# Two attention stages of a hybrid decoder layer written as one stage

## The reference, cut to what matters

```python
def mla_attend(q_lat, q_pe, segments):
    scores = []
    for c_kv, k_pe, mask in segments:
        s = (einsum('bqhc,bkc->bhqk', q_lat, c_kv)
             + einsum('bqhr,bkr->bhqk', q_pe, k_pe)) * SOFTMAX_SCALE
        scores.append(where(mask, s, -inf))
    p = softmax(concatenate(scores, axis=-1), axis=-1)
    # out: the sum over the segments of p times c_kv
```

## Time and profile before

| | us |
|---|---|
| median of 3 runs | 1552.9 (1550.19 to 1553.53) |
| the profiled execution's own time | 1556.86 |
| its span in the trace | 1555.2 |
| PE busy | 1470.7 (95%) |
| DVE busy | 810.7 (52%) |
| ACT busy | 582.2 (37%) |
| POOL busy | 389.4 (25%) |

### The profile page before, as it was taken

One profiled execution on the slowest core, in us unless ns is written; L12 is line 12 of the kernel. 1 busy time (PEld: TensorE's weight loads), 2 busy tenths in 40 slices (PEclk: granted clock), 3 DMA queues, 4 the chain that ended last, 5 costly groups with the idle time before them and its releaser, 6 DMA issues. The chain is left out here.

```text
span 1555.2 us, 26517 instructions
## 1 busy us (share of the span) xinstructions
PE 1470.7 (95%) x9613; PEld 1253.4 (81%) x9613; DVE 810.7 (52%) x1466; ACT 582.2 (37%) x1264; POOL 389.4 (25%) x520
## 2 busy tenths in 40 slices
PE   5999999999989988888999999999999998999997
PEld 4997777676767866555888999999999998787786
DVE  4512200054456654333148665666656665698877
ACT  4521112122333433222044544455444444443454
POOL 1136631040033002433000543433444342000000
PEclk9999999998989998997999999999999999999999
DMA  6431223343335001563232323332233335754764
GB/s 228 148 106 49 98 104 129 104 142 97 121 93 137 1 1 54 145 184 96 84 114 68 95 85 107 108 107 79 79 99 108 108 108 181 250 189 160 256 222 162
DMA packets 143279, 186.79 MB, mean 120 GB/s; under 512 B 22931, under 2 KB 89732, under 8 KB 142998
## 3 DMA queue, kind: packets, MB, share of 16 engines
q1 hardware_dynamic: 138382, 175.68, 35.2%
q0 software_dynamic: 4800, 9.84, 2.3%
HBM read 149.25 MB, written 36.19 MB: 119 GB/s over the span
## 5 line engine op out<-in xcount | busy, mean ns | idle before, releaser
L2939 PE MATMUL p_ff<-s_ff_th,s_ff_rhi 128*128 128x266 f32 x640 | 182.9, 286 | 0.4 <-ACT s_ff_u L2523 0.4
L2941 PE MATMUL p_ff<-s_ff_tl,s_ff_rhi 128*128 128x266 f32 x640 | 183.0, 286 | 0.0
L2942 PE MATMUL p_ff<-s_ff_th,s_ff_rlo 128*128 128x266 f32 x640 | 183.0, 286 | 0.0
L2939 PE MATMUL p_ff<-s_xh,s_ff_rhi 128*128 128x266 f32 x608 | 175.6, 289 | 5.4 <-DVE s_ff_rlo L2710 2.7
L2941 PE MATMUL p_ff<-s_xl,s_ff_rhi 128*128 128x266 f32 x608 | 174.2, 286 | 0.0
L2942 PE MATMUL p_ff<-s_xh,s_ff_rlo 128*128 128x266 f32 x608 | 173.9, 286 | 0.0
L118 PE MATMUL p_ip<-s_ip_hi,s_xh 128*128 128x512 f32 (+2 forms) x400 | 149.8, 375 | 3.6 <-DVE s_xl L216 3.6
L120 PE MATMUL p_ip<-s_ip_hi,s_xl 128*128 128x512 f32 (+2 forms) x400 | 148.8, 372 | 0.0
L119 PE MATMUL p_ip<-s_ip_lo,s_xh 128*128 128x512 f32 (+2 forms) x400 | 148.7, 372 | 0.0
L3044 PE MATMUL p_ff<-s_fd_wh,s_fd_ah 128*128 128x512 f32 x308 | 123.3, 400 | 8.2 <-DVE s_fd_wl L2818 4.3
L2939 PEld LDWEIGHTS p_ff<-s_xh,s_ff_rhi 128*128 128x128 f32 x608 | 114.9, 189 | 15.5 <-DVE s_ff_rlo L2710 8.5
(11 more groups left out here) (316 smaller groups left out, 3126.4 us busy)
## 6 DMA issues: line engine op xcount, KB each, us to landing
s_ff_raw<-in_w_up SPq DMA_DIRECT2D x44, 512.0 KB, 4.7
s_fd_lanes<-in_w_down SPq DMA_DIRECT2D x77, 256.0 KB, 3.4
s_fd_lanes<-a_rows SPq DMA_DIRECT2D x66, 256.0 KB, 3.3
a_rows<-s_ff_cv SPq DMA_DIRECT2D x22, 512.0 KB, 3.0
s_ff_scr<-in_w_down SPq DMA_DIRECT2D x11, 1024.0 KB, 6.1
s_ip_raw<-in_w_in SPq DMA_DIRECT2D x4, 2048.0 KB, 8.8
s_pages<-in_cache_kv_latent SPq DMA_DIRECT2D x56, 128.0 KB, 2.3
s_pages<-in_cache_kv_latent POOLq DMA_DIRECT2D x48, 128.0 KB, 2.5
```

The costliest lines, as they stand in the source:

```text
L2939: pe.matmul(out, rhi[:, s, ks_], hi_cols(k), start=first and k == 0, stop=False, skip_group_check=True)
L2941: pe.matmul(out, rhi[:, s, ks_], lo_cols(k), start=False, stop=False, skip_group_check=True)
L2942: mm = pe.matmul(out, rlo[:, s, ks_], hi_cols(k), start=False, stop=last and k == 3, skip_group_check=True)
```

## The change: what it does, and the diff

The two functions become one, `attention`, with one loop over k = 0..35. In step k it handles prompt item k and, for k < 32, cache page k (of four sequences). The other parts:

- The softmax of decode runs over blocks of 4 pages (8 blocks, 4 for each group) where it ran over segments of 8. Each block has its own maximum, exponential and rescaling of `total`. In step 4(B+1) block B gets maximum and exponential, one step later its transposes and `weigh`, and one step after that `take_part`.
- The pages lie in one ring of 8. Page n is loaded once `out_done` is n - 7, that is when `weigh` has passed page n - 8.
- The rotary keys of two sequences are transposed together, 128 columns wide, and multiplied from rows 0 to 63 and 64 to 127 of the matrix engine: 10 transposes for a page where there were 12.
- PSUM: 4 score banks as before, a ring of two banks for all transposes of both kinds (before: two in one stage, three in the other), one bank for the block's scores, and one bank that holds the two outputs of the prompt items and the output of the decode block (`misc`).
- Scores of decode are computed for 128 columns at a time, before for 256.
- SP issues its small transfers, two of them for the rotary queries, ahead of the first page. The first half of w_out is loaded once `weigh` has passed page 31, in step 33.

```diff
+NPG = 8
+BP = 4
+NBLOCK = DEC_B * NPAGE // (GB * BP)
+PAGES = NBLOCK * BP
 ...
+def attention(kit, t, x, spill, ident, w_uk, w_uv, qn_s, qp_s, kn, vt, qn, qp, kp, mh, ml, room, pages):
 ...
+        ring_b = kit.ps(c, "at_turn", 2)
+        mix_b = kit.ps(c, "at_mix", 1)
+        block_b = kit.ps(c, "at_block", 1)
 ...
+                sp.wait_ge(R["kept"], 2)
+                sp.dma_start(qpe_other[0:RO], qp_s[RO:P]).then_inc(R["q_low"], 16)
+                sp.dma_start(qpe_other[RO:P], qp_s[0:RO]).then_inc(R["q_low"], 16)
+                sp.wait_ge(pages.table, 16)
+                for n in range(NPG):
+                    pages.load_sync(sp, n)
 ...
+                for n in range(NPG, PAGES):
+                    sp.wait_ge(R["out_done"], n - NPG + 1)
 ...
+                    pages.load_sync(sp, n)
 ...
+                for k in range(NI):                      # ScalarE
+                    if k < PAGES:
+                        empty(act, place["keys", k, 0], copy)
+                    if k + 1 < NI:
+                        exp_part(k + 1)
+                    if block_at(k, 0) is not None:
+                        block_exp(block_at(k, 0))
+                    if k < PAGES:
+                        empty(act, place["keys", k, 2], copy)
 ...
+                def page_scores(n):                      # TensorE
+                    B, p = divmod(n, BP)
 ...
+                    wait_left(pe, place["keys", n, 1])
+                    wait_left(pe, place["keys", n, 2])
 ...
+                    if p == 0 and B:
+                        pe.wait_ge(R["exped"], B)
 ...
+                def weigh(B):
 ...
+                    wait_left(pe, place["probs", B])
+                    pe.wait_ge(S["lo_out"], BP * (B + 1) + 1)
 ...
-                for i in range(len(items)):
-                    if i + 1 < len(items):
-                        score_part(i + 1)
-                    if i:
-                        value_part(i - 1)
-                    turn_part(i)
+                for k in range(NI):
+                    if k + 1 < NI:
+                        score_part(k + 1)
+                    if k < PAGES:
+                        fill(place["keys", k, 0])
+                        fill(place["keys", k, 1])
+                    if k:
+                        value_part(k - 1)
+                    if k < PAGES:
+                        fill(place["keys", k, 2])
+                    B = block_at(k, 1)
+                    if B is not None:
+                        fill(place["probs", B])
+                        if last_of_group(B):
+                            fill(place["own", B])
+                    for n in turns(k):
+                        fill(n)
+                    if k < PAGES:
+                        page_scores(k)
+                        if (k + 1) % (GBLOCKS * BP) == 0:
+                            fill(place["self", k // (GBLOCKS * BP)])
+                    if B is not None:
+                        weigh(B)
+                    if closed(k) is not None:
+                        fill(place["close", closed(k)])
+                    if k and closed(k - 1) is not None:
+                        head_values(closed(k - 1))
```

More of the change, by code:

```diff
@@ L1163, in out_of @@
         def out_of(i):
[L1165 to L1196, removed]
@@ L1302, in _ @@
+                lo_part(NI - 1)
             @block.tensor
@@ L1784, in weigh @@
-                def weigh(s):
-                    g = s // HALVES
-                    for n in span("probs", s):
-                        wait_left(pe, n)
-                    if s and not has_own(s):
-                        pe.wait_ge(S["lo_out"], g)
-                        pe.wait_ge(S["o_out"], g)
-                    if has_own(s):
-                        pe.wait_ge(S["own_v"], 16 * (g + 1))
+                            r0 = RO * (b % 2) if paired and cc == 2 else 0
+                            w = qlat[:, cc, GB * g + b, :] if cc < 2 else qpe[r0:r0 + RO, GB * g + b, :]
@@ L1796, in weigh @@
                                       own_b[:, b, :], start=True, stop=False, skip_group_check=True,
                                       tile_position=(0, QR * b))
-                    for p in range(SEGP):
+                    for p in range(BP):
+                        n = B * BP + p
                         for b in range(GB):
-                            m = pe.matmul(misc_b[QR * b:QR * (b + 1), 0, 0:KVL], pt[:, p, QR * b:QR * (b + 1)],
-                                          pages.kv[s % 2][p][:, b, :], start=p == 0 and not has_own(s),
-                                          stop=p == SEGP - 1, skip_group_check=True, tile_position=(0, QR * b))
-                        m.then_inc(S["out_done"], 1)
@@ L1805, in close @@
-                def close(g):
-                    pe.wait_ge(S["normed"], g + 1)
-                    for cc in range(2):
-                        m = pe.transpose(misc_b[:, 0, cc * P:(cc + 1) * P], ol[:, cc * P:(cc + 1) * P], ident[:])
-                    m.then_inc(S["oturned"], 1)
-                    pe.wait_ge(S["o_out"], g + 1)
+                            m = pe.matmul(misc[QR * b:QR * (b + 1), :], dpt[:, p, QR * b:QR * (b + 1)],
+                                          pages.kv[n % NPG][:, b, :], start=p == 0 and not last_of_group(B),
+                                          stop=p == BP - 1, skip_group_check=True, tile_position=(0, QR * b))
@@ L1815, in close @@
                         for cc in range(2):
[L1816 to L1836 removed]
+                            m = pe.matmul(misc[:, h * n:(h + 1) * n], w_uv[:, cc, h, :],
+                                          rows_of[:, cc, :, h * DEC_T:(h + 1) * DEC_T], start=cc == 0, stop=cc == 1,
+                                          skip_group_check=True)
@@ new lines, in head_values, with latent_queries @@
+                    m.then_inc(R["uv"], 1)
+                def latent_queries():
+                    wait_left(pe, 1)
+                    pe.wait_ge(R["kept"], 2)
+                    for cc in range(2):
+                        for h in range(H):
+                            m = pe.matmul(misc[:, (cc * H + h) * NS:(cc * H + h + 1) * NS],
+                                          wukt[:, h, cc * P:(cc + 1) * P], qn_s[:, h, :], start=True, stop=True,
+                                          skip_group_check=True)
+                    m.then_inc(R["ql"], 1)
@@ L1840 @@
+                value_part(NI - 1)
 UW = DEC_B * (DEC_T + 2)
```

901 lines of the change are left out of this document (433 added, 468 removed).

## The result

The changed kernel takes 1540.2 us in the median of 18 runs (1535.2 to 1549.3), the kernel before 1551.2 in 18 runs beside them (1547.9 to 1554.0): ratio 0.9933, 95% interval 0.9919 to 0.9947, 11 us less. In three later sets the unchanged pair gave 0.9897, 0.9896 and 0.9913, 13 to 16 us less. Forecast were 31 to 34 us less. The direction is right and 1540 lies inside the range, but the size is a third to a half of the forecast.

The account below looks back on a forecast made before the run. TensorE was taken to bound both stages. Step 8 at 485, 173 us of work and 24.4 of waits end the joint stage at 682.8 instead of 716.7, 34 us less: 1523 profiled, 1520 us median, range 1500 to 1548.

Parts of the forecast that it names:

- the 675 to 693: Sign in the profile after: the joint stage was to end within these times, in us.
- First pages: Start of joint loop: page loads set the pace, SP's first page at 451.2, step 8 starting at 485.
- Steps 8 to 31: Part of steps 8 to 35 of the joint loop, forecast at 173.4 us of TensorE work, waits extra.
- the price of the scores by columns: TensorE scores: 2.58 ns a column for prompt items; 0.785 us a page, the lower bound against 1.57 by instructions.
- Waits: Added in the joint loop: 8.4 us for seven blocks, 5 us for hand-overs in 24 steps.
- The end: Pageless last four items wait 5 us, closing and barrier 2 us; joint stage ends at 682.8.
- Clock: Joint stage: one more stretch at 1.2 GHz of 8 us, costing 4 us.
- Pairs: Transposing rotary keys of two sequences together on TensorE saves 7.7 us (320 transposes against 384).
- The three signs: Would refute the prediction: page waits after step 12, page scores of 1.5 us, PEclk at 0.5 over 30 us.
- Nearly in series: Rival: TensorE's fixed order makes the joint loop wait on each step's chain; 12 to 15 us gained, 1539; chance 0.22.
- Slower by the clock: Rival: short waits keep TensorE at 1.2 GHz for 90 of the stage's 240 us; 1560 us; chance 0.12.
- no change: Rival: page scores go by instructions, 25 us more, and hand-overs cost 0.4 a step more; 1553; chance 0.04.
- deeper: Rival: joint stage hides all hand-overs, no 1.2 GHz stretch remains; 51 us gained at most, about 1504; chance 0.15.

Follow-up runs that it names:

- e_serial: Changed kernel with 36 more loop steps, each page worked on behind the last prompt item: 1576.6 us, ratio 1.0121 to the kernel before.
- Experiments 4 and 5: Changed kernel with prompt items reversed (1534.1 us), also w_out loadable earlier (1537.1), or pages four steps later (1533.3, again 1534.5) or two (1539.9).
- e_unpair: Changed kernel with each sequence's rotary keys transposed by itself, 4 transposes a page instead of 2: 1552.8 us, ratio 0.9973 to the kernel before.
- the two reverse orders: Changed kernel with prompt items in reverse order of blocks, 1534.1 us; the same with page buffers laid so w_out can load earlier, 1537.1 us.
- e_rev: Changed kernel with prompt items in reverse order of blocks, long ones first: 1534.1 us, ratio 0.9851 to the kernel before.

## Why the prediction was right or wrong

**What bounds the stage: right.** TensorE is busy 231 of 253.5 us, and no transfer is waited for.

**Total: wrong by 20 us in the median (1540.2 for 1520).** 13 of them are in the profiled execution (1536.3 for 1523), and 7 in what lies between it and the median, told below. In the profile, the stage's end was forecast at 682.8; ScalarE's first split of w_out, which stood at 716.7 before, stands at 696.5, 13.7 us later than forecast and past the 675 to 693 that were to show the prediction right. In order:

- *First pages.* Step 8 was to start at 485 and started at 486.3, but not for the reason given. SP's first issues in the changed kernel:

```profile
444.11 0.55 SPq L1361 DMA_DIRECT2D s_da_qpe_other<-s_qp_s  x1
444.70 0.60 SPq L1362 DMA_DIRECT2D s_da_qpe_other<-s_qp_s  x1
446.67 0.36 SPq L1160 DMA_DIRECT2D s_pages<-in_cache_kv_latent  x1
...
448.32 0.34 SPq L1160 DMA_DIRECT2D s_pages<-in_cache_kv_latent  x1
```

  The two rotary query transfers took 0.55 and 0.60 us, not the 2.13 of the earlier trace rows, and the first page went out at 446.7 instead of 451.2. The first transposes of a page stand at 452.9 (forecast not before 454), and TensorE waits for no page. From 442.5 to 486.3 are 43.8 us, of which the clock costs 0.46 x 13 + 0.05 x 15 = 6.7; the other 37 are TensorE's work and hand-overs, for which I had 29. One term was too dear and one too cheap, and the sum came out by chance. The Trainium skill (DMA: Bandwidth & Descriptors, "Issuing engines are not separate DMA queues") would have had TensorE set this part, and it does; still two page issues of SP lie 1.65 us apart, so the issue is not small, it only began early enough.
- *Steps 8 to 31: here it failed.* My terms give 146.6 us of work and 13.4 of waits, 160; the trace has 486.3 to 655.1, 168.8. From start to start, summed by line (transposes counted at their full-speed distance, 0.11 us and for the blocks 0.116; what their rows take beyond that is in the last line but one):

| | forecast | measured |
|---|---|---|
| prompt scores | 36.7 | 42.6 |
| values | 29.3 | 28.1 |
| prompt transposes | 14.5 | 14.5 |
| key transposes | 28.8 | 26.5 |
| page scores | 18.8 | 22.1 |
| six blocks, transposed and weighed | 13.6 | 14.0 |
| closing of group 0 and its own tokens | 4.9 | 2.9 |
| waits and hand-overs | 13.4 | 18.1 |
| sum | 160.0 | 168.8 |

  The failed step is **the price of the scores by columns, together with the hand-overs between the two kinds of work**. Of the 5.9 us at the prompt scores 1.9 are no error of the price: step k scores item k + 1, so these steps hold 752 columns more than I counted in them. The other 4.0 are. In nearly every step the first matmul of 512 columns takes 0.56 to 0.57 us to the next start where it took 0.46, now that page work in strips of 32 columns (128\*32 or 64\*32) stands ahead of it and not a transpose (128\*128). The items of 272 and 400 columns are 0.11 above the price too. The item of 912 columns, which gave the price in the earlier trace rows, before:

```profile
538.92 0.80 PE L1307 MATMUL p_pa_score<-s_kp,s_qp 128*128 128x512 f32 x1
```

  and now:

```profile
613.28 1.12 PE L1627 MATMUL p_at_score<-s_kn,s_qn 128*128 128x512 f32 x2
613.85 0.80 PE L1628 MATMUL p_at_score<-s_kp,s_qp 128*128 128x512 f32 x1
```

  The price counts the start at 538.46, 0.46 ahead; now it is 0.57. In the 24 steps that is some 2.5 us. In `e_serial`, where no page work stands between the items, it is 0.46 again (558.79 to 559.25, for one). Four items of 528 columns give most of the rest: each runs as 512 + 16. The trace of before has such an item:

```profile
487.38 0.29 PE L1306 MATMUL p_pa_score<-s_kn,s_qn 128*128 128x16 f32 x2
...
487.75 1.14 PE L1354 MATMUL p_pa_extra<-s_pa_pt,s_vt 128*128 128x128 f32 x8
```

  The 16 columns take 0.37 us (487.38 to 487.75) where the price gives 0.04: 1.3 us for the four. The pages' scores of 128 columns take 0.92 us a page instead of 0.785, 3.3 us in all; of the two bounds I had taken the lower for the whole. Key transposes and the closing came out 4.3 us too dear.
- *Waits.* 8.4 for the blocks and 5 for hand-overs were 4.7 us too little, counted from start to start. TensorE's idle time in these steps is only 8.8 us; the rest is what the last instruction ahead of a wait takes beyond the usual distance. Where they lie was half right: at prompt transposes that want a bank, less at the block's exponential.
- *The end.* 655.1 to 696.5 is 41.4 us; by my terms work 27, block 8 5, tail 2, clock 4: 38. Off by 3.6, and it was read as a fixed cost. Experiments 4 and 5 show that it isn't: it depends on which work stands beside the long items.
- *Clock.* I had 4 us for another stretch, and 0.20 x 20 = 4 us came, at the stage's end. But the first stretch I had counted as free, since pages were to set that part, and it costs 6.7. The stage lost 10.1 in all.'s middle stretch went, as much as some 5 us of the gain.
- *Pairs.* 7.7 forecast; 6.7 in instructions, 11 us in time: the shorter copy and the waits behind it were not counted.

Of the 13.7 us: 1.3 at the start, 8.8 in steps 8 to 31, 3.6 at the end. The three signs by which the prediction was to be known wrong (waits for pages, page scores of 1.5 us, more than 30 us at 0.5) all stayed away; none of them tested the terms that failed.

**The rivals.** "Nearly in series" was priced 1539 and the time came out at 1540, yet its mechanism is refuted: truly in series costs 35 us more, and in steps 8 to 31 TensorE is idle for 8.8 of 169 us. The agreement in time was chance. "Slower by the clock" fell (less time at 1.2 GHz, not more), and so did "no change" (0.92 us a page, not 1.57) and "deeper" (its 51 us would give 1502, not the 1504 that stands there). The rule that I weighed there (the Trainium skill, TensorE: Matmul & The Clock Gate, "A second HAM failure mode: psum-queue depth-cycling") speaks of a clock that keeps going up and down when PSUM banks are cycled through; here a loop over a ring of two banks has 1.00 for 210 us, so the trace disagrees for this loop.

**Profile against median.** I took the profiled execution as 4 us above the median, since that of before is. That of after was 4 us below its own. The runs differ mainly by the granted clock: of the 18 runs of the changed kernel the one of 1535.2 us had 0.983, the one of 1549.3 had 0.972, and a line through all has 11 us for each 0.01. In the second to fourth sets the kernel before has 0.973 on average and the changed one 0.978 to 0.980, which by that slope is 5 to 8 of the 13 to 16 us. That a third to a half of the gain is clock is worked out, not shown by an experiment: no run here fixes the clock. `e_unpair` has 0.979 on average, as the changed kernel (0.980 in that set), so what the pairs bring is not clock; but what it still gains on the kernel before, 5 us, is no more than its higher clock would give (0.006, some 7 us). What stays open is why the kernel before had 1551 us in the first set and 1557 to 1558 in the others.

## What to carry to other kernels

Price each shape that will run, the short remainders too, from a row of that shape, not by columns from the longest one, and price the change from one kind of work to the other. When two kinds of work are interleaved, look at what stands alone at either end: pages moved by four steps, without one instruction less, were worth 9 to 10 us where the whole change has 13 to 16 (in the second of the two sets some 3 of them by the clock, by the slope above). Undo the parts one by one before crediting the large idea: here the pairing, with two transposes instead of four and a shorter copy, gave most of the gain, and the joint order mainly paid for its own cost. And when banks are saved to make room, look at who now waits for whom: with two outputs in one bank TensorE waited 9.8 us where no other work stood between them.

## What the runs showed of the hardware

- A matmul instruction of 16 columns takes 0.07 to 0.12 us from start to start at a granted 1.00, about as long as a transpose of 128 columns (0.11).
- The first matmul of 512 columns takes 0.46 us to the next start behind a 128\*128 transpose, in all 20 such items of the kernel before and of `e_serial`. In the changed kernel it takes 0.56 to 0.57 behind work in strips of 32 columns, 17 of 20 items, and 0.46 in the two that have a transpose ahead (the last, behind the matmuls of the heads, has 0.54).
- The same kind of small transfer held SP for 2.13 us before and for 0.55 and 0.60 after, at another place in the program.
- The granted clock of 440 to 470, where the stage begins, is 0.89 and 0.94 in the two reverse orders, which begin with long prompt items. In all others it is lower: 0.60 in the serial kernel, 0.66 and 0.72 with pages from step 4 on, 0.72 to 0.83 in four profiles of the changed kernel, 0.77 in the kernel before, which has the same order of prompt items there as the serial one. So only the reverse orders stand out, and that long items are the reason is not shown. `e_rev` pays for it at its end, with 0.51 for 24 us.
